# A hybrid decoder step: constants loaded in two parts, three low parts of weights on VectorE, first projection pieces cut in halves

## The reference

```python
n = rmsnorm(x, norm_attn)                      # (1048, 1024)
z = n @ w_in                                   # (1024, 3072)
q, k, v, gb, gc, hc = jnp.split(z, SPLITS, axis=-1)
o = attend(q, k, v, lam)                       # differential attention, 4 heads, bias by distance
o = rmsnorm(o, attn_subln) * (1.0 - lam_init)
c_out = rmsnorm(gb * causal_conv(gc * hc), conv_norm)
h = x + jnp.concatenate([o, c_out], -1) @ w_out
y = h + hier_moe(rmsnorm(h, norm_ffn), ...)    # 4 groups of 8 experts, two of them for each token
```

## Time and profile before

| | us |
|---|---|
| timed runs | 1091.36 (1089.93, 1091.36, 1094.91) |
| profiled execution, its own time | 1087.63 |
| its span | 1085.8 |
| PE busy in the span | 937.0 (86%) |
| DVE, ACT, POOL busy | 569.8, 499.3, 465.1 |

### The profile page before, as it was taken

How to read it: one execution, slowest core, us unless ns; L and a number is a source line. 1 busy time by engine, 2 the same in 40 slices (tenths; PEclk the granted TensorE clock), 3 DMA queues, 4 the chain that set the end, 5 groups by cost and what they waited for, 6 DMA issues and landing times. The chain is left out here.

```text
span 1085.8 us, 14289 instructions
## 1 busy us (share of the span) xinstructions
PE 937.0 (86%) x5034; PEld 780.0 (72%) x5034; DVE 569.8 (52%) x1018; ACT 499.3 (46%) x828; POOL 465.1 (43%) x343
## 2 busy tenths in 40 slices
PE   3899999999999999967999999369999999999800
PEld 2799887887788778845788875358888887777600
DVE  3413533353326332667651136787777777667347
ACT  4333344334432434254221121548888877777412
POOL 3202223222322323248231121086999975655575
PEclk9899999999999999978897799579999999999955
DMA  8032321322110201543254321779999999998785
GB/s 242 23 91 92 97 78 59 120 89 88 40 61 20 58 25 38 164 143 107 77 199 129 105 81 59 314 274 376 404 408 410 406 406 398 403 387 351 275 292 208
DMA packets 92410, 206.25 MB, mean 190 GB/s; under 512 B 12751, under 2 KB 54159, under 8 KB 84150
## 3 DMA queue, kind: packets, MB, share of 16 engines
q1 hardware_dynamic: 80718, 171.37, 43.9%
q0 software_dynamic: 7008, 17.18, 4.4%
q10 hardware_dynamic: 4616, 16.80, 3.8%
HBM read 171.19 MB, written 42.34 MB: 197 GB/s over the span
## 5 line engine op out<-in xcount | busy, mean ns | idle before, releaser
L958 PE MATMUL pj<-n_hi,w_hi 128*128 128x350 f32 (+1 forms) x576 | 200.7, 348 | 5.2 <-DVE n_lo L1272 3.1
L1786 POOL TENSOR_TENSOR e_lo<-e_raw,e_hid 128x2048 fp32r<-128x2048 f32 x32 | 167.3, 5228 | 73.9 <-ACT e_hid L1782 73.8
L958 PE MATMUL pj<-n_lo,w_hi 128*128 128x350 f32 (+1 forms) x576 | 189.0, 328 | 0.0
L958 PE MATMUL pj<-n_hi,w_lo 128*128 128x350 f32 (+1 forms) x576 | 188.1, 327 | 0.0
L1786 DVE TENSOR_TENSOR e_lo<-e_raw,e_hig 128x2048 fp32r<-128x2048 f32 x64 | 148.1, 2316 | 0.1
L658 POOL TENSOR_TENSOR w_lo<-w_raw,w_hi 128x1024 fp32r<-128x1024 f32 x24 | 57.7, 2406 | 202.0 <-ACT w_hi L739 202.0
L958 PEld LDWEIGHTS pj<-n_hi,w_hi 128*128 128x128 f32 x576 | 110.2, 191 | 34.7 <-issue 32.7
L1782 ACT ACTIVATE e_hig<-e_raw 128x2048 fp32r<-128x2048 f32 x64 | 122.8, 1920 | 26.6 <-DMA e_raw<-in_w_up 19.7
L1234 DVE CUSTOM_DVE_ANT_0 sc<-pj,strip 128x512 f32<-128x512 f32 (+5 forms) x120 | 61.5, 545 | 100.4 <-PE pj L1024 63.8
L958 PEld LDWEIGHTS pj<-n_lo,w_hi 128*128 128x128 f32 x576 | 110.6, 192 | 0.6
L958 PEld LDWEIGHTS pj<-n_hi,w_lo 128*128 128x128 f32 x576 | 110.2, 191 | 0.7 <-issue 0.6
(11 more groups left out here) (256 smaller groups left out, 1808.7 us busy)
## 6 DMA issues: line engine op xcount, KB each, us to landing
e_raw<-in_w_up SPq DMA_DIRECT2D x32, 1024.0 KB, 17.4
e_raw<-in_w_gate SPq DMA_DIRECT2D x32, 1024.0 KB, 20.2
e_raw<-in_w_down SPq DMA_DIRECT2D x32, 1024.0 KB, 21.9
expert_rows<-yo ACTq DMA_DIRECT2D x32, 512.0 KB, 8.1
w_raw<-in_w_in SPq DMA_DIRECT2D x24, 512.0 KB, 3.9
expert_rows<-logits SPq DMA_DIRECT2D x16, 512.0 KB, 5.1
k_page<-in_cache_k SPq DMA_DIRECT2D x16, 256.0 KB, 3.7
wo_raw<-in_w_out SPq DMA_DIRECT2D x8, 512.0 KB, 3.5
```

What stands on the lines that cost most here:

```text
L958: ins = pe.matmul(pj[g % 2][:, 0:tn], ws[w][:, P * k:P * (k + 1)], x[:, k, t0:t0 + tn], start=(m == 0), stop=(m == 23))
L1786: eng.tensor_tensor(e_lo[r][:, q, :], e_raw[r][:, q, :], e_hi(par, q).bitcast(F32), ALU.subtract).then_inc(s_lo[q], 1)
```

## The change

`cst` is loaded in two DMAs: the identity and -0.5 (164 columns) with a semaphore of their own, for which PE and POOL wait, and the other 621 columns behind the weights of block 1, counted with the early loads. DVE waits for the gains alone. Tile 2 is loaded ahead of weights 0, tile 4 ahead of the early loads. The low parts of blocks 0, 1 and 2 are made by DVE, behind the low parts of tiles 1, 3 and 5, and no longer by POOL. ACT makes the high parts of blocks 0 and 1 one tile later, and evacuates piece 2 one tile later. PE works pieces 0, 1 and 2 in halves of 12 matmuls with one tile's transposes between and one behind; tiles 7 and 8 come ahead of the bias.

```diff
--- before.py
+++ after.py
@@ -80,6 +80,7 @@
 
     r = np.arange(P)
     put("ident", np.eye(P))
+    put("mhalf", np.full(NT * 4, -0.5))
     put("flip", np.eye(P)[::-1])
     put("before", (r[:, None] < r[None, :]).astype(np.float32))
     put("ones", np.ones(P))
@@ -93,7 +94,6 @@
     put("even", (r[:, None] % 2 == 0).astype(np.float32))
     put("odd", (r[:, None] % 2 == 1).astype(np.float32))
     put("pair", (r[:, None] // 2 == np.arange(32)[None, :]).astype(np.float32))
-    put("mhalf", np.full(NT * 4, -0.5))
     put("eps", [EPS])
     table = np.concatenate(cols, 1)
     dist = (STRIP - 1) - np.arange(GW)
@@ -143,6 +143,7 @@
             return ctx.enter_context(nc.psum_tensor(name, [P, 512], F32))
 
         cst = keep("cst", [P, NCST])
+        NFIRST = P + 4 * NT
 
         def C(name, rows=P):
             a, n = CAT[name if name != "iota32" else "iota128"]
@@ -275,6 +276,7 @@
         zero_row = logits[:].rearrange("p t c -> p (t c)")[:, 0:256]
         s_fill = sem("s_fill")
         s_const = sem("s_const")
+        s_first = sem("s_first")
         s_early = sem("s_early")
         s_x = [sem(f"s_x{i}") for i in range(3)]
         s_zero = sem("s_zero")
@@ -578,15 +580,16 @@
 
         def sync_ad(sp):
             load_x(sp, 0)
-            sp.dma_start(cst[:], c_table).then_inc(s_const, 16)
+            sp.dma_start(cst[:, 0:NFIRST], c_table[:, 0:NFIRST]).then_inc(s_first, 16)
             sp.dma_start(g_in[:], bass.AP(tensor=I["norm_attn"].tensor, offset=0, ap=[[0, P], [1, D]])).then_inc(s_const, 16)
             load_x(sp, 1)
+            load_x(sp, 2)
             load_w(sp, 0)
-            load_x(sp, 2)
             load_x(sp, 3)
             load_w(sp, 1)
+            sp.dma_start(cst[:, NFIRST:NCST], c_table[:, NFIRST:NCST]).then_inc(s_early, 16)
+            load_x(sp, 4)
             early_loads(sp)
-            load_x(sp, 4)
             load_w(sp, 2)
             for i in range(5, NT):
                 load_x(sp, i)
@@ -652,10 +655,10 @@
                         load_xr(sp, i + 2)
                     store_tile(sp, i)
 
-        def pool_low_w(pool, n):
-            pool.wait_ge(s_whi, n + 1)
+        def low_w(eng, n):
+            eng.wait_ge(s_whi, n + 1)
             w = w_slot(n)
-            pool.tensor_tensor(w_lo[w][:], w_raw[w][:], w_hi[w][:].bitcast(F32), ALU.subtract).then_inc(s_wlo, 1)
+            eng.tensor_tensor(w_lo[w][:], w_raw[w][:], w_hi[w][:].bitcast(F32), ALU.subtract).then_inc(s_wlo, 1)
 
         def pool_low_wo(pool, m):
             hi, lo = (wc_hi, wc_lo) if m < 4 else (wa_hi, wa_lo)
@@ -684,29 +687,27 @@
 
         def pool_ad(pool, did):
             pool.memset(c_ssum[:], 0.0).then_inc(s_cadd, 1)
-            pool.wait_ge(s_const, 32)
-            low_at = {1: 0, 2: 1, 5: 2}
+            pool.wait_ge(s_first, 16)
             for i in range(NT):
                 M = ROWS[i]
                 pool.wait_ge(s_ssq, i + 1)
                 did(pool.tensor_scalar(mean_eps[0:M, i:i + 1], ssq[0:M, i:i + 1], 1.0 / D, EPS, ALU.mult, ALU.add))
                 pool.wait_ge(s_pool, did.n[0])
                 pool.tensor_tensor(rstd[0:M, i:i + 1], mean_eps[0:M, i:i + 1], C("mhalf", M)[:, 0:1], ALU.pow).then_inc(s_rstd, 1)
-                if i in low_at:
-                    pool_low_w(pool, low_at[i])
-            pool_low_w(pool, 3)
+            pool.wait_ge(s_wlo, 3)
+            low_w(pool, 3)
             for s in range(SLOTS):
                 for g in (chunk_b(s - 1),):
                     for n in range(4, NB):
                         if g is not None and FIRST[n] - 2 == g:
-                            pool_low_w(pool, n)
+                            low_w(pool, n)
                 if (t := unit_at(s, 2)) is not None:
                     pool_root(pool, did, t)
                 if (h := head_at(s, 5)) is not None:
                     pool_cadd(pool, h)
                 for n in range(4, NB):
                     if chunk_a(s) is not None and FIRST[n] - 2 == chunk_a(s):
-                        pool_low_w(pool, n)
+                        low_w(pool, n)
                 for m in range(8):
                     if s == 32 + (m + 1) // 3:
                         pool_low_wo(pool, m)
@@ -816,16 +817,16 @@
                 for b in range(2):
                     act.wait_ge(s_trA, 2 * i + b + 1)
                     act.activation(n_hi[:, 4 * b:4 * b + 4, cols(i)], tp[b][:].rearrange("p (c t) -> p c t", c=4)[:, :, 0:M], ACT.Copy).then_inc(s_nhi, 1)
-                if i == 0:
+                if i == 1:
                     act_high_w(act, 0)
-                if i == 1:
+                if i == 2:
                     act_high_w(act, 1)
                 if i == 3:
                     act_after_chunk(act, 0)
                     act_high_w(act, 2)
                 if i == 5:
                     act_after_chunk(act, 1)
-                if i == 6:
+                if i == 7:
                     act_after_chunk(act, 2)
             for c in range(3):
                 a, b = 512 * c, min(GW, 512 * c + 512)
@@ -1045,18 +1046,16 @@
             ins.then_inc(s_dm, 1)
 
         def pe_ad(pe):
-            pe.wait_ge(s_const, 32)
+            pe.wait_ge(s_first, 16)
             ident = C("ident")
             for i in range(3):
                 pe_tr(pe, i)
-            pe_chunk(pe, 0, 0, 24)
-            pe_tr(pe, 3)
-            pe_chunk(pe, 1, 0, 24)
-            pe_tr(pe, 4)
-            pe_tr(pe, 5)
-            pe_chunk(pe, 2, 0, 24)
-            pe_tr(pe, 6)
-            pe.wait_ge(s_early, 16 * 12)
+            for g in range(3):
+                pe_chunk(pe, g, 0, 12)
+                pe_tr(pe, 2 * g + 3)
+                pe_chunk(pe, g, 12, 24)
+                pe_tr(pe, 2 * g + 4)
+            pe.wait_ge(s_early, 16 * 13)
             pe.wait_ge(s_zero, 1)
             for c in range(3):
                 a, b = 512 * c, min(GW, 512 * c + 512)
@@ -1064,10 +1063,7 @@
             for j in range(CJ):
                 ins = pe.transpose(pj[5][:, 16 * j:16 * (j + 1)], st_rows[:, P * j:P * (j + 1)], ident[0:16, 0:16])
             ins.then_inc(s_stT, 1)
-            pe_chunk(pe, 3, 0, 24)
-            pe_tr(pe, 7)
-            pe_tr(pe, 8)
-            for g in range(4, 7):
+            for g in range(3, 7):
                 pe_chunk(pe, g, 0, 24)
             pe_row_group(pe, "v", 0, 0)
             pe_row_group(pe, "v", 0, 1)
@@ -1252,7 +1248,7 @@
             did(dve.memset(u_ext[:, 0:2], 0.0))
             dve.wait_ge(s_step, did.n[0])
             dve.memset(cssq[:], 1.0).then_inc(s_zero, 1)
-            dve.wait_ge(s_const, 32)
+            dve.wait_ge(s_const, 16)
 
             def norm(i):
                 M = ROWS[i]
@@ -1271,7 +1267,10 @@
                     dve.wait_ge(s_nhi, 2 * i + b + 1)
                     dve.tensor_tensor(n_lo[:, 4 * b:4 * b + 4, cols(i)], tp[b][:].rearrange("p (c t) -> p c t", c=4)[:, :, 0:M],
                                       n_hi[:, 4 * b:4 * b + 4, cols(i)].bitcast(F32), ALU.subtract).then_inc(s_nlo, 1)
-            dve.wait_ge(s_early, 16 * 12)
+                for n, t in ((0, 1), (1, 3), (2, 5)):
+                    if t == i:
+                        low_w(dve, n)
+            dve.wait_ge(s_early, 16 * 13)
             did(dve.tensor_scalar(subln[:], subln[:], 1.0 - LAM_INIT, None, ALU.mult))
             did(dve.memset(logits[:], 0.0))
             dve.wait_ge(s_step, did.n[0])
```

## The result

The changed kernel took 1077.67 us (median of 9, 1073.81 to 1082.82), the kernel before beside it 1089.65 (median of 9, 1085.27 to 1094.91): ratio 0.9898, interval 0.987 to 0.9926, some 11 us less. A second set of 11 runs gave 1078.6 against 1088.31, ratio 0.9899 (0.9866 to 0.9932). The forecast was 1084.0 with a range from 1080 to 1089: faster, as said, but outside the range.

What follows compares the result with a forecast made beforehand. The first stage was taken as bound by no engine but by one chain round the engines for each tile; 3.2 + 5.2 - 0.5 - 0.5 = 7.4 us gave 1080.2 profiled, 1084.0 as median, range 1080 to 1089.

Steps and rivals of the forecast that it cites:

- The first term: Up to the start of piece 0 on PE: it starts at 21.6 instead of 24.8, a gain of 3.2 us.
- The second term: From piece 0 to piece 4: 5.2 us gained, 2.0 of idleness and 3.2 of the clock that did not fall.
- The new idle stretch before tile 5: In the middle of piece 1, PE idles 2.65 us until tile 5's transposes start at 33.85.
- the low part of weights 2 ends at 38.25, piece 2 at 38.4 (0.5 idle): Behind tile 6 on PE: piece 2 waits 0.5 us for DVE's low part of weights 2.
- POOL's root beside DVE's low part: Tile 3's root meets DVE's low part at 17.95 and is held: at most 0.65, 0.5 us deducted.
- a later rise of the clock: At piece 0 the clock may rise later than 3.1 us after its start: 0.5 us deducted.
- I let the gain run through to the end: Behind piece 4 each wait hangs on PE's own progress, so the gain of 7.4 us stays whole.
- The median of the timed runs lies 3.7 higher, at 1091.36: Step from profiled execution (1087.63 us before, 1080.2 forecast) to timed median, giving 1084.0.
- A: The clock falls again at the idle 2.65 us in piece 1, costing 3 to 3.7: 1087.4 us, chance 0.28.
- B: Behind piece 4 the gain is given back by late bias table, strip or weights 3: 1090 us, chance 0.13.
- C: Weights 0 land late and hold DVE's low part and tile 3's scaling: slower, 1093 us, chance 0.05.
- D: Tile 0's root still waits, for x; 0.9 is missing, 1084.9 us; chance counted within the forecast's 0.54.

Runs made afterwards that it cites:

- the squares ahead: The changed kernel with the squares of tiles 5 and 7 moved ahead of the evacuations of pieces 0 and 1 on ACT: 1076.22 us, ratio 0.9883.
- the low parts alone: The kernel before with only the low parts of weights 0 to 2 on DVE and the high parts one tile later: 1088.62 us, ratio 0.9997.
- table alone: The kernel before with only the table in two DMAs, own semaphores and the new order of loads: 1086.9 us, ratio 0.9973.
- table and halves: The changed kernel with the low parts of weights back on POOL and the high parts where they were: 1080.24 us, one time.
- table and low parts: The changed kernel with PE's order of before (pieces whole, tiles 4 and 5 in one row): 1088.4 us, one time.

## Why the prediction was wrong

The mechanism was right as far as piece 4: which waits go, and that the clock stays up before tile 5. **The first term** was 3.2 us and measured 3.11 (24.81 to 21.70; 3.9 between the second profiles). Its steps: root of tile 0 at 7.6, measured 6.59; square of tile 1 at 8.85, measured 9.43; transposes of tile 2 at 16.7, measured 16.16; low part on DVE 1.28, measured 1.22. The first root came a microsecond earlier than I had it, because tile 0 landed at 5.26 instead of 6.38; this is not the smaller table, since in the second profile of the kernel before, with the whole table, the square of tile 0 started at 5.16. DVE then waited for the gains, so most of it was not used. That the steps, up to a microsecond off either way, end within 0.1 us of the term is in part luck.

**The second term** was 5.2 us and measured 5.84 (35.67 less 29.83; 5.7 between the second profiles). The new idle stretch before tile 5 was put at 2.65 and measured 2.50; that before tile 7 at 1.25, measured 1.70. One step was false: "the low part of weights 2 ends at 38.25, piece 2 at 38.4 (0.5 idle)". Piece 2 is a piece of block 0 and needs the low part of weights 0 alone; PE went on from tile 6 (36.69) into it without a wait.

**The step that failed is the sum**, in three terms. Forecast and measured time are 6.3 us apart.

First, it took off 0.5 for POOL's root beside DVE's low part, and 0.5 for a later rise of the clock. Next to nothing of that came in this profile: the one such overlap was 0.14 us (the low part ends at 18.35, the root starts at 18.21), POOL's small operations took 192 ns, and the clock rose 3.6 us behind piece 0's start, against 3.2 before. Neither deduction was baseless: with the squares ahead, a POOL operation took 0.78 us beside a low part on DVE, and the clock rose 4.6 us behind piece 0 in the second profile of the changed kernel and 6.0 with the low parts alone. With these two, and the second term 0.6 too small, piece 4 was put 7.4 us earlier and came 8.95 earlier: 1.5 of the 6.3.

Second, "I let the gain run through to the end": from piece 4 to the end the changed kernel's profile was 2.2 us shorter, with fewer stretches at the low level. The term was put at nothing since the waits there move along, which they did; what differed was the clock, and two profiles of one kernel differ there by up to 3.9 us.

Third, and largest, "The median of the timed runs lies 3.7 higher, at 1091.36": I carried that distance over from three runs. Of the next comparisons the medians of the kernel before were 1088.3 to 1089.7, and the profiled execution of the changed kernel lay 1.2 below its median, in the second set 2.3 above it. That is 2.5 of the 6.3. From 1088.5, the summed terms give 1081.1; with the true 8.95, 1079.6; the two sets of the changed kernel measured 1077.67 and 1078.6. Where the last microsecond or two come from stays open; two profiles of one kernel differ by more. The range was drawn round a middle that was too high, and its lower end left 4 us for all of this.

**The rivals.** A did not come: behind 2.50 us the clock stayed up in both profiles of the changed kernel. Where the stretch was made longer (4.39) it fell, as A has it, and cost 1.28, not 3 to 3.7. B fell: PE behind piece 4 is as full as before. C fell: DVE waited 0.3 us in all for the high parts of weights. D fell: the root came 1.86 us earlier, of which DVE's wait for the gains left 1.26. Of the 1.86, 1.12 is tile 0's earlier landing; the table's share is that the root now starts 0.2 us behind the sum of squares instead of 0.9.

What I did not see is that the parts are worth little by themselves. I had priced them as links of one chain, each with its own share; the runs gave 0.9, 0.2 and 1.7 alone and 8.95 together (2.0, 1.3, 2.8 and 9.6 against the second profile of before), and the table next to nothing once the other two are there.

## What to carry to other kernels

In a chain that goes round over several engines, price an edit with the others in place, and try pairs before a part is thrown out for bringing nothing alone. Look for the operation that stretches when another engine runs beside it; one of 1.2 us on the right engine gave 3.4 us here, partly because the stretch decided whether the clock held. Which of two such operations starts first can decide which engine pays, so look at that order in more than one profile. And take the anchor of an absolute forecast from as many runs as there are: the difference of two profiles is better known than either time.

## What the runs showed of the hardware

- Where DVE's scaling, with two SBUF inputs, met POOL's low part, the one that started second was held. In eight cases (six profiles) DVE started 0.06 to 0.07 us behind POOL and took 3.35 to 3.37 us instead of 1.28; in three (before, table alone, table and halves) it started 0.4 to 0.5 us ahead and took 1.28, and POOL's low part took 3.01 to 3.13 instead of 2.35. The 3.36 are about POOL's 2.35 and 1.0 more, as if DVE stood until POOL was done.
- Before tile 5, idle stretches of PE of 2.49 to 2.65 us left the clock at 1.00 in four profiles; 3.33 to 4.75 us brought it down in six. There is no clean edge: of two stretches of 2.7 us before piece 1, one was followed by a fall and one was not, and the third fall with table and low parts, at 52.6 us, came with PE busy without a gap since 42.8, 2.3 us of it in six small matmuls (33x512) of the bias. The time at the low level was 3.4, 6.8 or 10.2 us.
- The tile loaded first was there at 5.10 to 5.66 us in 13 profiles and at 6.38 in one, the first of the kernel before, though it is issued first in all; a microsecond of a single profile's first stage can be chance.
